# The first modulation in two column halves, and eight projection units beside the second half

## The chip, the core and the metric

The program runs on one core of a Trainium2 chip. The metric is the device time of one execution in microseconds. A core has five engines that run their own instruction queues side by side and meet at semaphores: PE (TensorE) multiplies matrices into PSUM, DVE (VectorE) and POOL (GpSimd) do elementwise work, ACT (ScalarE) does functions and copies, and SP issues the DMAs. An engine takes its instructions strictly in the order in which they are written, so an instruction that waits holds back all that stands behind it.

## What is computed

Two transformer blocks over one sequence of 256 rows and 2048 columns, all in f32. The part that matters here is the start of the first block:

```python
mod = silu(c) @ w_ada + b_ada                      # 2048 -> 6 * 2048
shift1, scale1, gate1, shift2, scale2, gate2 = split(mod, 6)
h = rms(x, norm1_w) * (1 + scale1) + shift1
proj = h @ w_in                                    # 2048 -> 4096: u, q, k, v
y_ssm = s5_mixer(u, a, dt, b, c, d, w_glu)         # a state-space layer on the first 1024 columns
y_att = dilated_attention(q, k, v)
x = x + gate1 * (concat(y_ssm, y_att) @ w_out)
# then the feed-forward network, and the second block (latent attention and a Fourier mixer)
```

## The kernel before

The kernel streams all its weights once from HBM and is written as one ordered list of instructions for each engine.

**Projection units.** A weight matrix is cut into units of 256 rows by 512 columns (512 KB). `load` (L179) brings a unit into one of eight places of the ring `raw`; ACT rounds it to fp32r into `whi` (`high`, L185), DVE subtracts to get the rest `wlo` (`low`, L191), and PE runs 12 matmuls with it (`multiply`, L198): two row groups of the weight, two halves of the sequence, three products (high by high, high by low, low by high). `whi` and `wlo` have four places each, so unit u is rounded only when unit u - 4 was multiplied. The input projection `w_in` is 64 such units: eight column chunks in the order `IN_ORDER` (L1097), each eight units long. A chunk is stored from PSUM by `in_evac` (L1100).

**First modulation.** `shift1` and `scale1` are 4096 columns of `w_ada`. SP loads them as 64 slots of 512 KB (128 rows by 1024 columns) into `start_slots`, eight places of SBUF of their own (`slots_sp`, L236). PE consumes two slots a round (`rounds_pe`, L246), 32 rounds; each round is four matmuls of 512 columns on four column groups of the array. A slot is loaded again when the round that used it is over. When all 32 rounds are done, ACT copies the sums (`set_row_act`, L275), PE turns them into columns (`set_turn_pe`, L281), and DVE adds the bias (`set_store_dve`, L295). The sums of the four pairs of columns come complete only together, with the last round.

**Turning h.** The normalized x is transposed on PE in eight steps r of two row groups (`turn_pe`, L400), DVE applies scale and shift (`turn_dve`, L412), ACT rounds to `hh` (`turn_act`, L425), and POOL subtracts to `hl` (`turn_pool`, L430). The projection starts when all eight are done (L2716).

**State-space tables.** Beside this, DVE prepares the state-space layer: parameters (L519), the table `W` (`windows_dve`, L592), which stands in `raw`, and the read tables `ct` (`reads_dve`, L607), which stand in `x` and `araw`. PE transposes `W` (`window_turn_pe`, L654) in 16 groups that ACT stores (L664), and multiplies it with `cpad` (`kt4_pe`, L669), 2 times 32 small matmuls, that ACT stores with 10 copies each (`kt4_act`, L679). SP starts the first units of `w_in` when PE has done with `W` (L2600 and L2601), since they land in the same memory.

**After the first chunks.** The first two chunks are u of the state-space layer. `u_turn_pe` (L701) transposes them, ACT and DVE copy them (`u4_act`, `u4_dve`), `ends_pe` (L731) multiplies, `ends_act` stores, and POOL runs a recurrence over the sequence (`scan`, L748), once for each half b. `y_pe` (L790) for half 0 stands behind unit 38 on PE and waits for that scan. The order of PE around the change is the body at L2702 to L2718 and `in_pe` (L1135).

## Time and profile before

| | us |
|---|---|
| median of 3 runs | 2775.4 (2774.17 to 2776.24) |
| the profiled execution | 2773.86 |
| its span | 2772.0 |
| PE busy | 2555.9 (92% of the span) |
| DVE busy | 1627.1 (59%) |
| ACT busy | 1035.2 (37%) |
| POOL busy | 204.7 (7%) |
| mean granted TensorE clock | 0.955 |

The span is the time from the first to the last instruction of the profiled execution; 1.9 us of its time lie around it. The page gives busy shares over the whole span. The change touches the first 260 us, so the stretches of that part are read apart, engine by engine in order of time. Granted clock 1.00 means 2.4 GHz and 0.50 means 1.2 GHz; a value between them is a stretch that has both.

### The profile page before, as it was taken

What the parts mean: (1) busy time and instruction counts of PE and PEld (TensorE: products, weight loads), DVE (VectorE), ACT (ScalarE), POOL (GpSimd) and SP (SyncE); (2) the same over time, 40 slices, a digit from 0 to 9 for tenths busy, and PEclk for the clock granted to TensorE, in tenths of its full rate; (3) what the DMA queues carried; (4) which work ended last, traced back from release to release, by engine and by line L of the source; (5) the groups of instructions that cost most, each with busy time, mean ns of one, the idle gap of its engine ahead of it and who ended that gap; (6) DMA issues with size and microseconds to landing.
All of it is one profiled execution on the core that took longest, in us unless ns stands there. A gap on an engine that the chain in (4) does not pass through costs nothing. (4 is left out here: it accounts for less than half of the span.)

```text
span 2772.0 us, 30616 instructions
## 1 busy us (share of the span) xinstructions
PE 2555.9 (92%) x11822; PEld 1957.1 (71%) x11822; DVE 1627.1 (59%) x1909; ACT 1035.2 (37%) x1354; POOL 204.7 (7%) x192
## 2 busy tenths in 40 slices
PE   5899887979999999999989999998949999999994
PEld 1588665547777777778768877776837777877773
DVE  8454534346777777875775674444563564744446
ACT  1343653224333333333434554443323333333331
POOL 0126800010000000000101000000020000000000
PEclk9799899989999999999999999998969999999996
DMA  9654458957999999995545643331444665745530
GB/s 392 249 152 129 131 210 321 377 206 272 339 343 342 337 343 354 357 341 180 162 152 170 203 137 99 99 122 55 158 159 143 210 225 171 270 144 153 150 118 30
DMA packets 277473, 589.24 MB, mean 213 GB/s; under 512 B 20304, under 2 KB 29264, under 8 KB 275792
## 3 DMA queue, kind: packets, MB, share of 16 engines
q1 hardware_dynamic: 277328, 587.28, 61.5%
q8 instruction: 94, 1.54, 0.2%
q14 instruction: 51, 0.42, 0.0%
HBM read 585.11 MB, written 2.10 MB: 212 GB/s over the span
## 5 line engine op out<-in xcount | busy, mean ns | idle before, releaser
L195 DVE TENSOR_TENSOR wlo<-raw,whi 128x1024 fp32r<-128x1024 f32 (+2 forms) x728 | 882.0, 1227 | 716.7 <-ACT whi L189 705.4
L189 ACT CAST whi<-raw 128x1024 fp32r<-128x1024 f32 (+2 forms) x728 | 738.0, 1024 | 978.6 <-PE psum L208 902.2
L206 PE MATMUL psum<-whi,hh 128*128 128x512 f32 (+1 forms) x2080 | 842.4, 405 | 40.1 <-DVE wlo L195 39.5
L208 PE MATMUL psum<-whi,hl 128*128 128x512 f32 (+1 forms) x2080 | 818.7, 394 | 0.0
L207 PE MATMUL psum<-wlo,hh 128*128 128x512 f32 (+1 forms) x2080 | 816.6, 393 | 0.0
L206 PEld LDWEIGHTS psum<-whi,hh 128*128 128x128 f32 x2080 | 395.6, 190 | 165.6 <-issue 76.5
L208 PEld LDWEIGHTS psum<-whi,hl 128*128 128x128 f32 x2080 | 395.0, 190 | 88.5
L207 PEld LDWEIGHTS psum<-wlo,hh 128*128 128x128 f32 x2080 | 395.8, 190 | 82.7 <-issue 2.6
L206 PE MATMUL psum<-whi,hidh 128*128 128x512 f32 x608 | 249.6, 411 | 7.7 <-DVE wlo L195 6.0
L207 PE MATMUL psum<-wlo,hidh 128*128 128x512 f32 x608 | 242.4, 399 | 0.0
L208 PE MATMUL psum<-whi,hidl 128*128 128x512 f32 x608 | 242.4, 399 | 0.0
L343 DVE SCALAR_TENSOR_TENSOR powers<-araw,cond,powers 128x512 f32<-128x512 f32 x300 | 225.2, 751 | 14.4 <-DVE powers L343 0.5
L398 POOL TENSOR_TENSOR rstd<-ms,mhalf 128x2 f32<-128x2 f32 x7 | 4.9, 699 | 2137.6 <-DVE ms L387 1843.6
L206 PEld LDWEIGHTS psum<-whi,hidh 128*128 128x128 f32 x608 | 115.5, 190 | 45.2 <-issue 16.2
L207 PEld LDWEIGHTS psum<-wlo,hidh 128*128 128x128 f32 x608 | 115.5, 190 | 29.7 <-issue 3.1
L208 PEld LDWEIGHTS psum<-whi,hidl 128*128 128x128 f32 x608 | 115.5, 190 | 28.1
L1542 DVE TENSOR_TENSOR xacc<-xacc,psum 128x1024 f32<-128x1024 f32 x68 | 82.9, 1219 | 35.8 <-PE psum L208 35.8
L266 PE MATMUL psum<-start_slots,cond_windows 128*32 128x512 f32 x256 | 49.4, 876 | 34.8 <-DMA start_slots<-in_w_ada 34.8
L408 PE MATMUL psum<-ident,xacc 128*128 128x128 f32 x128 | 29.3, 383 | 49.2 <-DVE xacc L393 29.5
L408 PEld LDWEIGHTS psum<-ident,xacc 128*128 128x128 f32 x128 | 21.0, 195 | 57.6 <-DVE xacc L393 30.0
L1635 PE MATMUL psum<-dft,ub 128*128 128x512 f32 x128 | 57.8, 594 | 2.4 <-DVE ub L1523 1.3
L428 ACT CAST hh<-h 128x512 fp32r<-128x512 f32 x32 | 19.9, 621 | 104.7 <-DVE h L421 104.7
(330 smaller groups left out, 2127.4 us busy)
## 6 DMA issues: line engine op xcount, KB each, us to landing
araw<-in_ada_w SPq DMA_DIRECT2D x128, 512.0 KB, 6.6
raw<-in_w_in_fourier SPq DMA_DIRECT2D x128, 512.0 KB, 4.3
raw<-in_w_ffn_gate SPq DMA_DIRECT2D x88, 512.0 KB, 9.6
raw<-in_w_ffn_up SPq DMA_DIRECT2D x88, 512.0 KB, 7.7
raw<-in_w_ffn_down SPq DMA_DIRECT2D x88, 512.0 KB, 10.1
raw<-in_w_in_attn SPq DMA_DIRECT2D x88, 512.0 KB, 4.1
araw<-in_w_ada SPq DMA_DIRECT2D x80, 512.0 KB, 6.4
start_slots<-in_w_ada SPq DMA_DIRECT2D x64, 512.0 KB, 7.7
```

What stands on the lines that cost most here:

```text
L189: nc.scalar.copy(whi[:, u % SPLITS, 0:kn, 0:w], raw[:, u % RING, 0:kn, 0:w]).then_inc(s_hi, 1)
L195: nc.vector.tensor_tensor(wlo[:, u % SPLITS, 0:kn, 0:w], raw[:, u % RING, 0:kn, 0:w], whi[:, u % SPLITS, 0:kn, 0:w].bitcast(F32), ALU.subt ...
L206: nc.tensor.matmul(o, ah[:, kt + k, a], h, start=(kt + k == first_kt), stop=False)
L207: nc.tensor.matmul(o, ah[:, kt + k, a], lw, start=False, stop=False)
L208: ins = nc.tensor.matmul(o, al[:, kt + k, a], h, start=False, stop=(kt + k == last_kt))
L266: ins = nc.tensor.matmul(psum[32 * g:32 * g + 32, SET_BANKS[st][0]], condz[:, vectors - 1, kt, 3 - pi:35 - pi], slot(2 * r + e)[0][:, half ...
L343: ins = nc.vector.scalar_tensor_tensor(out=dst, in0=w, scalar=s, in1=dst, op0=ALU.mult, op1=ALU.add)
L398: nc.gpsimd.tensor_tensor(rstd[:], ms[:], mhalf[:, 0:2].unsqueeze(2), ALU.pow).then_inc(s_rs, 1)
L408: ins = nc.tensor.transpose(psum[:, banks[r % 2], j * S + t * P:j * S + t * P + P], xn[:, t, kt * P:(kt + 1) * P], ident[:])
L428: nc.scalar.copy(oh[:, 2 * r:2 * r + 2], h32[:, r % 2]).then_inc(s_hh, 1)
L1542: nc.vector.tensor_tensor(o, o, psum[:, BANK[n]:BANK[n] + 2], ALU.add).then_inc(H.dv, 1)
L1635: ins = nc.tensor.matmul(psum[:, 2 + half], ub[:, t, g * S + half * P:g * S + half * P + P], dft[:, t], start=(t == 0), stop=(t == TT - 1))
```

## The change

- `PE_PAIRS` and `PE_SETS`: the 32 rounds become two sets of 16. The first set is columns 1024 to 2047 of shift and of scale, the second is columns 0 to 1023. Each set has its own row copy, turn and store (`first_columns_dve`).
- The turn of h is split: steps for row groups 8 to 15 follow the first set (`turned` swaps the halves), those for row groups 0 to 7 follow the second.
- `IN_FIRST`: of the first two chunks, the eight units on row groups 8 to 15 come first (units 0 to 7), then the eight on row groups 0 to 7 (units 8 to 15). Both chunks are open in PSUM at once.
- Homes: slots of the first modulation land in `raw`, units 0 to 7 in `araw`; `W` stands in `proj` and `bt_x` in three pieces, where its transposes also go; `cpad` stands in `proj`, and the scratch of the read tables in `ptmp`. With `W` in three pieces, each operation on it becomes three instructions.
- Order: `windows_dve` and `reads_dve` are cut into steps that stand between the units on DVE. On PE the units 0 to 7, the two `kt4_pe` and the 16 window transposes stand between the rounds 16 to 31. `in_evac` for the first two chunks waits for the tables. The u transposes move from behind units 12 and 20 to behind 16 and 22, `ends_pe` from 16 and 24 to 19 and 25.

```diff
     raw = sb(ctx, "raw", [P, RING, 2, CW])
-    a1 = ExitStack()
-    start_slots = sb(a1, "start_slots", [P, 8, 2 * CW])
-    a1.close()
     whi = sb(ctx, "whi", [P, SPLITS, 2, CW], F32R)
     wlo = sb(ctx, "wlo", [P, SPLITS, 2, CW], F32R)
...
+    def landing(u):
+
+        return araw[:, u % 4] if u < RING else raw[:, u % RING]
+
     def load(sp, u, src, w=CW, per=0, i=None):
         kn = src.shape[1]
         if i is not None or u >= RING:
             sp.wait_ge(s_lo, at(u - RING + 1, per, i))
-        sp.dma_start(raw[:, u % RING, 0:kn, 0:w], src).then_inc(s_raw[u % RING], 16)
+        elif u >= 4:
+            sp.wait_ge(s_lo, u - 3)
+        if RING <= u < 2 * RING:
+            sp.wait_ge(s_aused, 29 + (u - RING) // 2)
+        sp.dma_start(landing(u)[:, 0:kn, 0:w], src).then_inc(s_raw[u % RING], 16)
...
-    PE_PAIRS = (0, 1, 2, 3, 4, 5, 6, 7, 8, 9, 12, 13, 14, 15)
-    PE_SETS = ((0, 4, 1), (4, 2, 1), (6, 4, 1), (10, 4, 2))
-    SET_BANKS = ((6, 7), (6, 7), (6, 7), (7, 7))
+    PE_PAIRS = (1, 3, 0, 2, 4, 5, 6, 7, 8, 9, 12, 13, 14, 15)
+    PE_SETS = ((0, 2, 1), (2, 2, 1), (4, 2, 1), (6, 4, 1), (10, 4, 2))
+    SET_BANKS = ((6, 7), (6, 7), (6, 7), (6, 7), (7, 7))
...
-            t = start_slots[:, b]
+            t = raw[:, b].rearrange("p a b -> p (a b)")
...
+    def turned(k, r):
+
+        return (r + 4) % 8 if k == 0 else r
...
     btmp = pre[:, 3072:4096].rearrange("p (g c) -> p g c", g=PAIRS)
-    cpad = pre[:, 4096:6144].rearrange("p (r g c) -> p r g c", r=2, g=PAIRS)
-    ctmp = pre[:, 6144:8192].rearrange("p (g d c) -> p g d c", g=16, d=4)
-    W = rawf.rearrange("p (r g i c) -> p r g i c", r=2, g=PAIRS, i=4)
+    wtmp = pre[:, 1024:2048].rearrange("p (g c) -> p g c", g=PAIRS)
+    cpad = proj[:, :, 0:1024].rearrange("p r (g c) -> p r g c", g=PAIRS)
+    ctmp = ptmp[:].rearrange("p (g d c) -> p g d c", g=8, d=4)
+    W = (proj[:, :, 1024:3072].rearrange("p t (g r i c) -> p t g r i c", g=8, r=2, i=4),
+         proj[:, :, 3072:4096].rearrange("p t (g r i c) -> p t g r i c", g=4, r=2, i=4),
+         bt_x[:].rearrange("p (t g r) (i c) -> p t g r i c", t=1, r=2, i=4))
...
-    def windows_dve(dve, ch):
+    def windows_dve(dve, ch, i):
 
         V = nc.vector
-        br, bi = W[:, 0, :, 3], W[:, 1, :, 3]
-        for i in range(3):
-            ar, ai = (apow[:, q, :, 2 - i:3 - i].broadcast_to([P, PAIRS, 2 * GCH]) for q in range(2))
-            for q, (u, v, op) in enumerate(((br, bi, ALU.subtract), (bi, br, ALU.add))):
-                ch(V.tensor_tensor(W[:, q, :, i], ar, u, ALU.mult))
-                ch(V.tensor_tensor(btmp, ai, v, ALU.mult))
-                ch.wait()
-                ins = V.tensor_tensor(W[:, q, :, i], W[:, q, :, i], btmp, op)
+        ar, ai = (apow[:, q, :, 2 - i:3 - i].broadcast_to([P, PAIRS, 2 * GCH]) for q in range(2))
+        for q, op in enumerate((ALU.subtract, ALU.add)):
+            for n in range(3):
+                ch(V.tensor_tensor(W[n][:, :, :, q, i], of_pairs(ar, n), W[n][:, :, :, q, 3], ALU.mult))
+                ch(V.tensor_tensor(of_pairs(wtmp, n), of_pairs(ai, n), W[n][:, :, :, 1 - q, 3], ALU.mult))
+            ch.wait()
+            for n in range(3):
+                ins = V.tensor_tensor(W[n][:, :, :, q, i], W[n][:, :, :, q, i], of_pairs(wtmp, n), op)
                 ch(ins)
-                ch.wait()
-        V.tensor_copy(neg[:, 0:1], W[:, 0, 0, 0, 0:1]).then_inc(s_W, 1)
-
-    def reads_dve(dve, ch):
+            ch.wait()
+        if i == 2:
+            V.tensor_copy(neg[:, 0:1], cols[:, 0:1]).then_inc(s_W, 1)
...
     def window_turn_pe(pe, g0, g1):
-        pe.wait_ge(s_W, 1)
         for g in range(g0, g1):
-            if g >= 4:
-                pe.wait_ge(s_bt4, g - 3)
+            if g < 2:
+                pe.wait_ge(s_kt4, g + 1)
+            else:
+                pe.wait_ge(s_bt4, g - 1)
             for j in range(4):
-                ins = nc.tensor.transpose(psum[:, g % 4, j * P:(j + 1) * P], W[:, j % 2, 2 * g + j // 2]
-                                          .rearrange("p i c -> p (i c)"), ident[:])
+                ins = nc.tensor.transpose(psum[:, 4 + g % 2, j * P:(j + 1) * P], bt4(2 * g + j // 2, j % 2), ident[:])
             ins.then_inc(s_wt, 1)
...
+    IN_FIRST = ((0, 4), (1, 4), (0, 5), (1, 5), (0, 6), (1, 6), (0, 7), (1, 7),
+                (0, 0), (1, 0), (0, 1), (0, 2), (0, 3), (1, 1), (1, 2), (1, 3))
+
+    def in_unit(n):
+
+        return IN_FIRST[n] if n < 16 else (n // UPC, n % UPC)
+
     IN_ORDER = (0, 1, 2, 4, 6, 3, 5, 7)
     IN_BANK = (0, 2, 0, 2, 0, 6, 4, 6)
 
     def in_evac(act, o):
         c = IN_ORDER[o]
-        act.wait_ge(s_mm, U_IN + UPC * (o + 1))
+        act.wait_ge(s_mm, U_IN + (UPC * (o + 1) if o else 13))
+        if o < 2:
+            act.wait_ge(s_ct, 2)
+            act.wait_ge(s_ktp, 2)
         if o in (2, 4):
             act.wait_ge(s_L, o // 2)
         nc.scalar.copy(proj[:, :, c * CW:(c + 1) * CW], psum[:, IN_BANK[o]:IN_BANK[o] + 2]).then_inc(s_inev, 1)
 
     def in_load(sp, n):
-        c = IN_ORDER[n // UPC]
-        load(sp, U_IN + n, w_rows(dram["w_in"][0], 2 * (n % UPC), 2)[:, :, c * CW:(c + 1) * CW])
+        o, j = in_unit(n)
+        c = IN_ORDER[o]
+        load(sp, U_IN + n, w_rows(dram["w_in"][0], 2 * j, 2)[:, :, c * CW:(c + 1) * CW])
 
     def in_mult(pe, n):
-        o, j = n // UPC, n % UPC
-        if j == 0 and o >= 2:
+        o, j = in_unit(n)
+        if o < 2:
+            pe.wait_ge(s_hl, (j + 4) % 8 + 1)
+            multiply(pe, U_IN + n, lat(IN_BANK[o]), 2 * j, 7, first_kt=8)
+            return
...
     def in_pe(pe):
-        for n in range(43):
+        for n in range(10, 43):
             in_mult(pe, n)
             for b in range(2):
-                if n == 12 + 8 * b:
+                if n == 16 + 6 * b:
                     u_turn_pe(pe, b)
-                if n == 16 + 8 * b:
+                if n == 19 + 6 * b:
                     ends_pe(pe, b)
             if n == 38:
...
-            if n >= UPC and n % UPC == 3:
+        for n in range(12, 42):
+            if n == 15:
+                in_evac(act, 0)
+            if n >= 2 * UPC and n % UPC == 3:
                 in_evac(act, n // UPC - 1)
             for b in range(2):
-                if n == 16 + 8 * b:
+                if n == 19 + 6 * b:
                     u4_act(act, b)
-                if n == 20 + 8 * b:
+                if n == 23 + 6 * b:
                     ends_act(act, b)
             high(act, U_IN + n)
...
-                if n == 15 + 8 * b:
+                if n == 18 + 6 * b:
                     u4_dve(dve, b)
...
-        slots_sp(sp, 0, 4)
+        slots_sp(sp, 0, 2)
         sp.dma_start(x[:], dram["x"][0].rearrange("(t p) n -> p t n", p=P)).then_inc(s_x, 16)
-        sp.dma_start(pre[:, 4096:6144].rearrange("p (r n) -> p r n", r=2), dram["c_pad"].rearrange("r p n -> p r n")).then_inc(s_cpad, 16)
-        slots_sp(sp, 4, 64)
-        sp.wait_ge(s_wt, 16)
-        sp.wait_ge(s_ktp, 2)
+        slots_sp(sp, 2, 32)
+        sp.dma_start(proj[:, :, 0:1024], dram["c_pad"].rearrange("r p n -> p r n")).then_inc(s_cpad, 16)
+        in_load(sp, 0)
+        in_load(sp, 1)
+        slots_sp(sp, 32, 36)
+        in_load(sp, 2)
+        in_load(sp, 3)
+        for k in range(4, 8):
+            slots_sp(sp, 20 + 4 * k, 24 + 4 * k)
+            in_load(sp, k)
+        slots_sp(sp, 52, 64)
         in_sp(sp)
...
+        set_row_act(act, 0)
+        for r in range(4):
+            turn_act(act, 0, h32, hh, r, r + 1)
+            if r % 2:
+                high(act, U_IN + r // 2)
         act.wait_ge(s_cpad, 16)
         nc.scalar.mul(cpad[:, 1], cpad[:, 1], -1.0).then_inc(s_cneg, 1)
+        high(act, U_IN + 2)
+        high(act, U_IN + 3)
+        kt4_act(act, 0)
+        high(act, U_IN + 4)
+        high(act, U_IN + 5)
+        kt4_act(act, 1)
+        high(act, U_IN + 6)
+        high(act, U_IN + 7)
         window_turn_act(act)
-        kt4_act(act, 0)
-        kt4_act(act, 1)
-        set_row_act(act, 0)
-        act.wait_ge(s_ct, 2)
-        act.wait_ge(s_ktp, 2)
-        turn_act(act, 0, h32, hh)
+        act.wait_ge(s_hl, 4)
+        set_row_act(act, 1)
+        for r in range(4, 8):
+            turn_act(act, 0, h32, hh, r, r + 1)
+            high(act, U_IN + 4 + r)
         in_act(act)
...
-        windows_dve(dve, ch)
         norm_dve(dve, ch, 0, x, xn, True)
-        reads_dve(dve, ch)
-        set_store_dve(dve, 0)
-        dve.wait_ge(s_mcol, 1)
-        ch(nc.vector.scalar_tensor_tensor(out=mscale[:], in0=modc[:, 16:32], scalar=1.0, in1=cols[:, COLS["n1"]],
-                                          op0=ALU.add, op1=ALU.mult))
-        ch.wait()
-        turn_dve(dve, 0, h32, mscale, modc[:, 0:16])
+        windows_dve(dve, ch, 0)
+        windows_dve(dve, ch, 1)
+        first_columns_dve(dve, ch, 0)
+        for r in range(4):
+            turn_dve(dve, 0, h32, mscale, modc[:, 0:16], r, r + 1)
+            if r % 2:
+                low(dve, U_IN + r // 2)
+        windows_dve(dve, ch, 2)
+        low(dve, U_IN + 2)
+        low(dve, U_IN + 3)
+        reads_dve(dve, ch, 0, 0)
+        low(dve, U_IN + 4)
+        low(dve, U_IN + 5)
+        reads_dve(dve, ch, 0, 1)
+        low(dve, U_IN + 6)
+        low(dve, U_IN + 7)
+        first_columns_dve(dve, ch, 1)
+        for r in range(4, 8):
+            turn_dve(dve, 0, h32, mscale, modc[:, 0:16], r, r + 1)
+            low(dve, U_IN + 4 + r)
+            if r == 5:
+                reads_dve(dve, ch, 1, 0)
+        reads_dve(dve, ch, 1, 1)
         in_dve(dve, ch)
...
-        rounds_pe(pe, 0, 16)
-        for k in range(4):
-            window_turn_pe(pe, 4 * k, 4 * k + 4)
+        rounds_pe(pe, 0, 14)
+        turn_pe(pe, 0, xn, 0, 0, 2)
+        rounds_pe(pe, 14, 16)
+        set_turn_pe(pe, 0)
+        turn_pe(pe, 0, xn, 0, 2, 4)
+        for k in range(2):
             rounds_pe(pe, 16 + 2 * k, 18 + 2 * k)
+            in_mult(pe, 2 * k)
+            in_mult(pe, 2 * k + 1)
         kt4_pe(pe, 0)
-        rounds_pe(pe, 24, 27)
+        rounds_pe(pe, 20, 21)
+        in_mult(pe, 4)
         kt4_pe(pe, 1)
-        rounds_pe(pe, 27, 32)
-        set_turn_pe(pe, 0)
-        pe.wait_ge(s_kt4, 2)
-        turn_pe(pe, 0, xn, 0)
-        pe.wait_ge(s_hl, 8)
+        in_mult(pe, 5)
+        rounds_pe(pe, 21, 23)
+        in_mult(pe, 6)
+        in_mult(pe, 7)
+        for k in range(8):
+            window_turn_pe(pe, 2 * k, 2 * k + 2)
+            rounds_pe(pe, 23 + k, 24 + k)
+        rounds_pe(pe, 31, 32)
+        pe.wait_ge(s_bt4, 16)
+        turn_pe(pe, 0, xn, 0, 4, 6)
+        set_turn_pe(pe, 1)
+        turn_pe(pe, 0, xn, 0, 6, 7)
+        in_mult(pe, 8)
+        turn_pe(pe, 0, xn, 0, 7, 8)
+        in_mult(pe, 9)
```

On PE, before, from the last window transposes to the end of the rounds (L660 transposes `W`, L675 is `kt4_pe`, L266 is four matmuls a round):

```order
L660 MATMUL psum<-ident,raw 128x128 x16
L266 MATMUL psum<-start_slots,cond_windows 32x512 x8
L675 MATMUL psum<-ssm_preparation,raw 128x32 x32
L266 MATMUL psum<-start_slots,cond_windows 32x512 x12
L675 MATMUL psum<-ssm_preparation,raw 128x32 x32
L266 MATMUL psum<-start_slots,cond_windows 32x512 x20
L291 MATMUL psum<-select,h 128x4 x8
```

On PE, now, the same stretch from behind units 2 and 3 (L211 to L213 are a unit's matmuls, here units 4 to 7; L713 is `kt4_pe`, L271 the rounds, L698 the window transposes; what is left out repeats its neighbours):

```order
L713 MATMUL psum<-proj 128x32 x32
L271 MATMUL psum<-raw,cond_windows 32x512 x4
L211 MATMUL psum<-whi,hh 128x512
...
L713 MATMUL psum<-proj 128x32 x16
L713 MATMUL psum<-proj,bt_x 128x32 x16
L211 MATMUL psum<-whi,hh 128x512
...
L271 MATMUL psum<-raw,cond_windows 32x512 x8
L211 MATMUL psum<-whi,hh 128x512
...
L698 MATMUL psum<-ident,proj 128x128 x8
L271 MATMUL psum<-raw,cond_windows 32x512 x4
```

Three rounds stood between the two `kt4_pe`, and now one round and one unit do. Of the 16 rounds of the second set, nine now stand behind unit 7: eight behind two groups of window transposes each, and then the last one.

On ACT, before, from the sign change of `cpad` to the first units (L685 is `kt4_act`, L667 stores the window transposes):

```order
L2641 ACTIVATE ssm_preparation<-ssm_preparation 128x1024
L667 COPY proj<-psum 128x512 x12
L667 COPY bt_x<-psum 128x512 x4
L685 COPY kt<-psum 32x16x32 x20
L279 COPY h<-psum 128x512
L428 CAST hh<-h 128x512 x8
L189 CAST whi<-raw 128x1024 x11
```

On ACT, now (L194 is `high`, L723 `kt4_act`, L704 the window stores):

```order
L2719 ACTIVATE proj<-proj 128x1024
L194 CAST whi<-araw 128x1024 x2
L723 COPY kt<-psum 32x16x32 x10
L194 CAST whi<-araw 128x1024 x2
L723 COPY kt<-psum 32x16x32 x10
L194 CAST whi<-araw 128x1024 x2
L704 COPY proj<-psum 128x512 x12
```

The casts of units 4 and 5 stand behind the ten copies of the first `kt4`, those of units 6 and 7 behind the second ten.

On DVE, now, behind the second set of columns (L438 is a step of h, L200 `low`, L648 to L656 half a read table; before, both whole tables stood ahead of the modulation's columns):

```order
L438 TENSOR_SCALAR h<-psum,mscale,modc 128x256 x2
L200 TENSOR_TENSOR wlo<-raw,whi 128x1024
L648 TENSOR_TENSOR araw<-powers,proj 128x1024
L649 TENSOR_TENSOR pool_scan_tmp<-powers,proj 128x1024
L651 TENSOR_TENSOR araw<-araw,pool_scan_tmp 128x1024
L652 TENSOR_TENSOR araw<-powers,proj 128x1024
L654 TENSOR_TENSOR pool_scan_tmp<-powers,proj 128x1024
L656 TENSOR_TENSOR araw<-araw,pool_scan_tmp 128x1024
L438 TENSOR_SCALAR h<-psum,mscale,modc 128x256 x2
L200 TENSOR_TENSOR wlo<-raw,whi 128x1024
```

Half a read table now stands between `low` of unit 9 and the step of h that unit 11 needs, ahead of `low` of unit 10; the other half stands ahead of `low` of unit 12.

## Rows read from the trace of the kernel before

**Rows 1.** Busy time by stretch: PE, PEld, DVE, ACT, POOL; granted clock, DMA share, GB/s.

```profile
60.00:80.00 20.00, 15.50 (x129) 8.13 (x126) 19.76 (x10) 7.46 (x15) 0.00 (x0) 1.00 1.03 409
80.00:100.00 20.00, 20.00 (x122) 15.98 (x121) 9.63 (x5) 5.79 (x10) 0.00 (x0) 0.66 0.71 263
100.00:120.00 20.00, 17.11 (x95) 10.33 (x94) 2.85 (x8) 7.62 (x13) 1.97 (x2) 0.67 0.66 240
140.00:160.00 20.00, 20.00 (x89) 16.43 (x88) 9.28 (x8) 8.29 (x8) 0.00 (x0) 1.00 0.65 185
```

**Rows 2.** Timeline of PE to 115 us: start, length, instructions, idle before and releaser.

```profile
56.23 1.94 PE L266 MATMUL psum<-start_slots,cond_windows 128*32 128x512 f32 x8 [1.50 <-DMA start_slots<-in_w_ada]
...
60.48 1.93 PE L266 MATMUL psum<-start_slots,cond_windows 128*32 128x512 f32 x16
62.34 1.97 PE L660 MATMUL psum<-ident,raw 128*128 128x128 f32 x16
...
78.79 10.02 PE L675 MATMUL psum<-ssm_preparation,raw 128*128 128x32 f32 x64
88.73 5.01 PE L266 MATMUL psum<-start_slots,cond_windows 128*32 128x512 f32 x24
93.68 11.14 PE L675 MATMUL psum<-ssm_preparation,raw 128*128 128x32 f32 x64
...
111.91 1.07 PE L266 MATMUL psum<-start_slots,cond_windows 128*32 128x512 f32 x8 [0.77 <-DMA start_slots<-in_w_ada]
113.67 1.95 PE L291 MATMUL psum<-select,h 128*128 128x4 f32 x16 [0.70 <-ACT h L279]
```

**Rows 3.** Timeline of the DMA issues on SP, the last 60 slots.

```profile
5.43 102.12 SPq L244 DMA_DIRECT2D start_slots<-in_w_ada  x60
```

**Rows 4.** Timeline of DVE.

```profile
31.10 1.21 DVE L599 TENSOR_TENSOR raw<-powers,raw 128x1024 f32<-128x1024 f32 x1
...
53.09 4.84 DVE L371 BATCH_NORM_STATS2 stat<-x 128x6 f32<-128x512 f32 x8
...
62.35 2.29 DVE L616 TENSOR_TENSOR x<-powers,ssm_preparation 128x2048 f32<-128x2048 f32 x1
...
129.49 4.86 DVE L195 TENSOR_TENSOR wlo<-raw,whi 128x1024 fp32r<-128x1024 f32 x4 [1.63 <-ACT whi L189]
...
169.43 3.49 DVE L718 COPY proj<-psum 32x256 f32<-32x256 f32 x8 [4.00 <-PE psum L710]
```

**Rows 5.** Timeline of ACT.

```profile
88.84 5.90 ACT L685 COPY kt<-psum 32x512 f32<-32x512 f32 x10 [12.43 <-PE psum L675]
...
117.34 0.62 ACT L428 CAST hh<-h 128x512 fp32r<-128x512 f32 x1 [3.71 <-DVE h L421]
...
138.39 1.05 ACT L189 CAST whi<-raw 128x1024 fp32r<-128x1024 f32 x1 [1.69 <-PE psum L208]
...
154.81 1.02 ACT L1105 COPY proj<-psum 128x1024 f32<-128x1024 f32 x1 [1.64 <-PE psum L208]
...
187.52 1.93 ACT L746 COPY xacc<-psum 128x1024 f32<-128x1024 f32 x2 [7.88 <-PE psum L739]
```

**Rows 6.** Timeline of POOL: two steps of h, first and last instruction of scan 0.

```profile
121.14 2.50 POOL L433 TENSOR_TENSOR hl<-h,hh 128x512 fp32r<-128x512 f32 x2 [0.61 <-ACT hh L428]
...
189.53 0.88 POOL L767 TENSOR_TENSOR pool_scan_tmp<-powers,xacc 128x256 f32<-128x256 f32 x1 [59.67 <-ACT xacc L746]
...
253.73 1.75 POOL L786 TENSOR_TENSOR xacc<-xacc,pool_scan_tmp 128x784 f32<-128x784 f32 x1
```

**Rows 7.** Timeline of PE: unit 0, two of its matmuls, start of `y_pe` 0.

```profile
131.09 0.76 PE L206 MATMUL psum<-whi,hh 128*128 128x512 f32 x1 [5.17 <-DVE wlo L195]
...
132.50 0.63 PE L206 MATMUL psum<-whi,hh 128*128 128x512 f32 x1
132.93 0.63 PE L207 MATMUL psum<-wlo,hh 128*128 128x512 f32 x1
...
256.01 0.33 PE L799 MATMUL psum<-proj,kt 128*128 128x64 f32 x2
```

More of the change, by code:

```diff
@@ L754, in scan @@
         pool.wait_ge(s_H, 2 * b + 2)
+        pool.wait_ge(s_ct, 2)
         if b:
@@ L1123, in in_sp @@
     def in_sp(sp):
-        for n in range(8 * UPC):
+        for n in range(8, 8 * UPC):
             in_load(sp, n)
```

122 lines of the change are left out of this document (77 added, 45 removed).

## The prediction

> **What bounds the kernel now.** I read the page first: PE is busy 92% of the span, so a stretch pays only as far as it moves PE's work. Then the busy time by stretch. From 140 to 160 us PE is busy in all 20 us at granted clock 1.00 (2.4 GHz), and the DMA engines have air (share 0.65) [rows 1]. Before that three things follow each other. Until 80 us the DMA is full (share 1.00, 409 GB/s); from 80 to 120 us it is at 0.66 to 0.71 and PE is busy nearly throughout, at clock 0.66 [rows 1]. The timeline of PE says with what: the two `kt4_pe` take 10.02 and 11.14 us, and the rounds between them wait in line [rows 2]. The last round ends at 112.98 (111.91 + 1.07) [rows 2], SP having issued the last slot at 107.55 (5.43 + 102.12) [rows 3]. Third, the turn of h: from 115.6 until unit 0 starts at 131.09 PE mostly waits [rows 2, 7]. I take as the marks of the kernel before: unit 8 starts about 154.3 (the store of chunk 0, released by unit 7, starts at 154.81) [rows 5], and `y_pe` 0 starts at 256.01 [rows 7]. From there both programs have the same order, so the shift of `y_pe` 0 is the change of the time.
>
> **What the change would save.** Units 0 to 7 leave the path: 8 x 2.75 us (a unit's cast is followed by a wait of 1.69 us after 1.05 us [rows 5], and PE has no gap, so 2.75 a unit) = 22 us, and half of the turn of h. It adds to the DMA ahead of the last round 8 units of 512 KB, at 409 GB/s 1.28 us each, 10 us. That is paid if PE comes to its rounds in time. I therefore follow the three engines through the new order.
>
> **DVE up to W.** It decides when units 2 and 3 can be multiplied, since their `low` stands behind the third window step. Parameters end at 31.1 as before [rows 4]. An instruction of 1024 elements takes 1.21 us and one of 2048 takes 2.29, so the fixed part is about 0.13. The new homes add 8 instructions to the parameters and 12 to each window step: 1.0 and 1.6 us. The window steps took 22.0 us together (31.1 to 53.09), 7.3 each, now 8.9; the norm took 9.3 (53.09 to 62.35) [rows 4]. Norm done 41.4, two windows 59.2. Meanwhile round 15 is over: it was at 58.2 [rows 2], less 2.6 for `c_pad` (1 MB), which is now issued later; its row copy and turn (0.6 and 2.0 us, [rows 2]) end about 58.4. So both meet at 59, and the wait for columns is nothing. Four steps of h go at the pace of POOL, whose pair takes 2.50 us behind an idle 0.61, 3.1 us for two steps [rows 6], and two `low` (1.22 us each, [rows 4]) stand between, each behind a cast of 1.05: about 10 us, to 69. Third window step 78.0, `low` 2 done 79.2.
>
> **PE up to the last round.** From 79.2 the order on PE is serial, and each item has a row:
> units 2 and 3, 6.5 (5.5 at 2.75; at the low clock a matmul starts every 0.43 us (132.50, 132.93 [rows 7]), 5.1 a unit; PE waited just before, so I take a good third of the difference for one of them) -> 85.7;
> `kt4_pe` 0, 10.0 [rows 2] -> 95.7;
> then unit 4, whose cast stands behind the ten copies of `kt4_act` 0: 5.90 + 1.05 [rows 5] + `low` 1.22 + three handovers of 0.1 = 8.5, round 20 lying inside -> 104.2; unit 4 itself 3.9 (middle of 2.75 and 5.1) -> 108.1;
> `kt4_pe` 1, 11.1 [rows 2] -> 119.2;
> again 8.5 for `kt4_act` 1, cast and `low` of unit 6; unit 5 and rounds 21 and 22 (4.7 to 8.4 us) lie inside -> 127.7;
> units 6 and 7, 6.5 -> 134.2;
> 64 window transposes at 0.123 us (1.97 for 16 [rows 2]) 7.9, and eight rounds at 0.97 (1.93 for two) to 1.67 (5.01 for three) [rows 2], I take 1.3: 10.4 -> 152.5;
> the last round, whose slots were issued only when a place came free, 2.0 -> 154.5.
> Before it was 112.98. The slots wait all this time for PE; the DMA, which was the bound to 80 us, is idle for half of it. So the change turns a stretch in which loading hid the table work on PE into one in which table work, ACT's copies and units stand in one chain.
>
> **From the last round to unit 8.** Row copy and turn, 2.7 with handover (112.98 to 115.6 [rows 2]), columns 0.5, h 1.0, `hh` 0.62 [rows 5], cast 1.05, `low` 1.22, handovers 0.4: 7.5. Unit 8 at 162.0, 7.7 later than before.
>
> **From unit 8 to `y_pe` 0.** Both programs have units 8 to 38, two u transposes and two `ends_pe` in this stretch: 101.7 us before (154.3 to 256.0), without a wait. The new order adds:
> two single steps of transposes on PE, 1.0;
> half a read table (six instructions of 1024, 7.4) ahead of `low` 10: from unit 8's start DVE needs h 1.0, `hh` and cast and `low` 9 2.9 with handovers, table 7.4, h 1.0, `hh`, cast and `low` 10 2.9 = 15.2, while PE has units 8 and 9 and the transposes, about 7: wait 8;
> the other half ahead of `low` 12: 3.9 for `low` 11, 7.4, 1.3 = 12.6, against units 10 and 11 at 5.5 to 7.5: wait 5 to 7, I take 5;
> the u copies of DVE (3.49 [rows 4]) and a `low` now have only one unit between the transposes and the unit that needs it (4.8 - 2.75): 2.0, twice. Before there were two units, 5.5 us of cover;
> scan 0 took 66.0 us (189.53 to 255.48 [rows 6]) and ended 0.5 us before PE came to `y_pe` 0 [rows 7]: no slack. It starts 2.1 us after `ends_pe` (187.4; the store starts at 187.52 [rows 5]). PE now has three units fewer between the two: 68.5 - 8.25 + 2.0 (second u wait) = 62.3 against 68.1: wait 5.8;
> low clock after these waits, two units, half of it: 2.4.
> Together 26. Where I cost the rest at nothing (loads of units 0 to 7, `cpad` later, `high` beside), it is because these land or end before 79 us, when DVE is what is late.
>
> **Sum.** 7.7 + 25.9 = 33.5 us. The profiled execution has 2773.9 us, of which 1.9 around its span; 2773.9 + 33.5 = 2807. (The median of the runs shown is 1.5 us above that execution.)
>
> **A rule against the row.** Clock: kt4's stretch shows 0.66, although PE is busy 20.00 of 20 us, and unit 0 starts at 0.43 us a matmul after an idle stretch [rows 1, 7]. The Trainium skill, TensorE: Matmul & The Clock Gate, Part 1 (What's actually happening), says that the throttled state is the default and that activity releases it. By that rule the first unit behind every one of the six long waits would run at 1.2 GHz throughout, 2.35 us each, 14 us instead of the some 6 that stand in the sum, 2815; with the clock low all through the chain it is rival C. At unit 0 the trace agrees for the matmuls shown, and at the next units it has the pace of 2.75 again [rows 5, 7], so the sum goes by the rows.
>
> **Rivals.**
> A, faster: the loads stay the bound. PE does its table work in the gaps between slots, and the last round follows the DMA: 24 rounds were over at 78.8 before, eight more at 2.56 (two slots at 1.28) make 99.3, and the eight unit loads 109.5. Unit 8 at 117.0, 37.3 earlier; less the 25.9 behind it gives 11.4 faster, 2762. For it: PE had a gap of 1.50 us ahead of round 15 [rows 2], and a DMA share of 0.7 from 80 us on shows loading time to be had [rows 1]. Against it: the written order puts `kt4_pe` ahead of eleven rounds and behind W, which is ready at 78. It decides at the last round: break-even is 154.3 - 25.9 - 7.5 = 121, that is a chain of 42 us behind `low` 2 where I count 75.
> B, small loss: the front as I have it or 4 us shorter, and the waits behind unit 8 mostly overlapped (the table halves fall into waits for `hl`, the scan runs faster when DVE is idle): 5 + 10, 2789. For it: from 80 us on DVE was busy for only 9.63 of 20 us and then 2.85 [rows 1], so there is room beside PE's chain. Against it: the halves are placed exactly where PE needs DVE, and the scan's length is measured.
> C, larger loss, clock at 1.2 GHz through the chain: units 2 to 4, 6 and 7 at 5.1 instead of 16.9 in all +8, rounds +3, units behind the waits +6: 2824. For it: rows 1, 80 to 120.
>
> **How the numbers follow.** Forecast 0.67, A 0.11, B 0.14, C 0.08. The forecast's own range: `kt4_pe` at the high clock at best half, 5 us each, is -10; rounds at 0.97, -3; all units at 2.75, -4; extra fixed costs on DVE at nothing, -5: all together 2785, and upward rounds and units at the low clock and the second table's wait at 7: 2820. The range for 8 in 10: 2785 to 2825. Within 0.2% (5.5 us, about what can be told from no change) 0.03, a corner of A and B; faster 0.11; slower 0.86.
>
> **What would show it.** Right: the last round near 154 (over 135 in any case); PE waiting 6 to 7 us for `low` ahead of unit 4, and again ahead of unit 6 for 1 to 4; a DMA share well under 0.7 between 85 and 150; waits of 8 and 5 us ahead of units 10 and 12; 5 us ahead of `y_pe` 0, released by POOL; from there on the same distances as before. Wrong: the last round before 121, or unit 8 before 145; or equal marks at `y_pe` 0.

## The result, and the profile after

The changed kernel takes 2813.8 us (median of 4, 2812.3 to 2815.5) against 2774.8 before (median of 4, 2773.9 to 2776.2): ratio 1.014, interval 1.0123 to 1.0158. Its profiled execution has 2815.3 us and a span of 2813.5, 41.5 more than before; the forecast was 2807. One execution of the kernel with the casts ahead, below, took 11190.7 us, four times as long as any other, and is left out of its median.

| | before | after |
|---|---|---|
| span | 2772.0 | 2813.5 |
| PE busy | 2555.9 | 2567.2 |
| DVE busy | 1627.1 | 1628.8 |
| mean granted clock | 0.955 | 0.947 |
| last round ends | 112.98 | 161.27 |
| unit 8 starts | 154.62 | 168.71 |
| `y_pe` 0 starts | 256.01 | 295.64 |

PE is busy 11.3 us longer only, and the span grew by 41.5: 30.2 of the loss is idle time of PE, and the other 11.3 go with a lower mean clock and hardly with added work (11838 matmul records for 11822). 39.6 of it stand at the start of `y_pe` 0. The stretches that answer to [rows 1], same columns:

```profile
60.00:80.00 20.00, 14.25 (x67) 7.63 (x66) 16.60 (x30) 6.84 (x9) 5.03 (x4) 0.76 1.03 404
80.00:100.00 20.00, 18.49 (x94) 15.34 (x92) 6.68 (x6) 3.28 (x6) 0.00 (x0) 0.67 0.29 106
100.00:120.00 20.00, 14.93 (x73) 13.80 (x73) 9.45 (x8) 4.48 (x7) 0.00 (x0) 0.59 0.13 49
120.00:140.00 20.00, 14.32 (x54) 9.97 (x54) 2.45 (x2) 7.86 (x12) 0.00 (x0) 0.76 0.36 131
140.00:160.00 20.00, 17.76 (x132) 9.17 (x130) 0.00 (x0) 8.59 (x16) 0.00 (x0) 0.96 0.77 284
```

Read the DMA share first. To 80 us it is full in both kernels. From 80 to 140 it is 0.29, 0.13 and 0.36 now, where it was 0.71, 0.66 and 0.45 before (the first two in [rows 1], the third here; the last slot was issued at 107.55 there): the loading of the second half, which the eight units were to lie beside, all but stands still.

```profile
120.00:140.00 20.00, 13.37 (x49) 10.08 (x50) 12.00 (x17) 9.63 (x12) 8.02 (x7) 0.64 0.45 148
```

In the same stretches of the changed kernel PE is busy 18.5, 14.9 and 14.3 of 20 us, and DVE and ACT are idle for most of it: they take turns. The timeline of PE names the turns (answers to [rows 2, 7]):

```profile
78.61 0.77 PE L211 MATMUL psum<-whi,hh 128*128 128x512 f32 x1 [4.17 <-DVE wlo L200]
...
86.50 10.12 PE L713 MATMUL psum<-proj 128*128 128x32 f32 x64
...
105.07 0.76 PE L211 MATMUL psum<-whi,hh 128*128 128x512 f32 x1 [6.58 <-DVE wlo L200]
...
110.32 3.93 PE L713 MATMUL psum<-proj 128*128 128x32 f32 x32
114.09 6.82 PE L713 MATMUL psum<-proj,bt_x 128*128 128x32 f32 x32
...
129.35 0.47 PE L211 MATMUL psum<-whi,hh 128*128 128x512 f32 x1 [2.00 <-DVE wlo L200]
...
136.03 0.77 PE L211 MATMUL psum<-whi,hh 128*128 128x512 f32 x1 [3.67 <-DVE wlo L200]
...
141.28 1.20 PE L698 MATMUL psum<-ident,proj 128*128 128x128 f32 x8
...
160.20 1.07 PE L271 MATMUL psum<-raw,cond_windows 128*32 128x512 f32 x8 [1.49 <-DMA raw<-in_w_ada]
...
168.71 0.77 PE L211 MATMUL psum<-whi,hh 128*128 128x512 f32 x1 [1.99 <-DVE wlo L200]
...
184.00 0.77 PE L211 MATMUL psum<-whi,hh 128*128 128x512 f32 x1 [7.42 <-DVE wlo L200]
...
196.44 0.77 PE L211 MATMUL psum<-whi,hh 128*128 128x512 f32 x1 [4.19 <-DVE wlo L200]
...
217.63 0.50 PE L211 MATMUL psum<-whi,hh 128*128 128x512 f32 x1 [2.07 <-DVE wlo L200]
...
245.12 0.47 PE L211 MATMUL psum<-whi,hh 128*128 128x512 f32 x1 [2.66 <-DVE wlo L200]
...
295.64 0.41 PE L838 MATMUL psum<-proj,kt 128*128 128x64 f32 x2 [1.81 <-POOL xacc L825]
```

DVE is named ahead of unit 4 (6.58 us), but DVE had waited 16.91 us for ACT itself, and ACT had stood at the ten copies of `kt4`. Of ACT, then of DVE:

```profile
96.66 5.88 ACT L723 COPY kt<-psum 32x512 f32<-32x512 f32 x10 [26.50 <-PE psum L713]
102.56 1.99 ACT L194 CAST whi<-araw 128x1024 fp32r<-128x1024 f32 x2
120.94 5.88 ACT L723 COPY kt<-psum 32x512 f32<-32x512 f32 x10 [16.39 <-PE psum L713]
126.85 1.04 ACT L194 CAST whi<-araw 128x1024 fp32r<-128x1024 f32 x1
133.58 1.04 ACT L194 CAST whi<-araw 128x1024 fp32r<-128x1024 f32 x1 [5.69 <-DMA araw<-in_w_in]
```

```profile
103.69 2.36 DVE L200 TENSOR_TENSOR wlo<-araw,whi 128x1024 fp32r<-128x1024 f32 x2 [16.91 <-ACT whi L194]
```

The last cast, of unit 7, waited 5.69 us for its load. SP shows why (answers to [rows 3]):

```profile
98.55 28.81 SPq L249 DMA_DIRECT2D raw<-in_w_ada  x4
127.40 0.43 SPq L188 DMA_DIRECT2D araw<-in_w_in  x1
127.88 24.67 SPq L249 DMA_DIRECT2D raw<-in_w_ada  x12
```

The first of these rows merges slots 48 to 51. Slots 48 and 49 were issued at 98.55, when round 20 was over. Slots 50 and 51 waited until 126.56 for round 21, which stands on PE behind unit 5, and the load of unit 7 stands behind them in SP's queue. Its place in memory was free from `low` of unit 3 on, at 79.6.

### The profile page after: what moved, and what is told of

It is laid out like the page before. It is cut to its first block and busy times, and to the rows that moved or that the text cites. A ratio compares the mean times of both kernels' runs of the same rounds, so it can differ in the third digit from the quotient of the medians.

```text
span 2813.5 us, 30735 instructions
## 1 busy us (share of the span) xinstructions
PE 2567.2 (91%) x11838; PEld 1966.1 (70%) x11838; DVE 1628.8 (58%) x1969; ACT 1032.6 (37%) x1355; POOL 201.7 (7%) x192
## 5 line engine op out<-in xcount | busy, mean ns | idle before, releaser
L200 DVE TENSOR_TENSOR wlo<-raw,whi 128x1024 fp32r<-128x1024 f32 (+2 forms) x720 | 869.2, 1223 | 712.7 <-ACT whi L194 706.9
L194 ACT CAST whi<-raw 128x1024 fp32r<-128x1024 f32 (+2 forms) x720 | 727.5, 1021 | 965.1 <-PE psum L213 878.6
L211 PE MATMUL psum<-whi,hh 128*128 128x512 f32 (+1 forms) x2080 | 848.1, 408 | 71.2 <-DVE wlo L200 70.7
L213 PE MATMUL psum<-whi,hl 128*128 128x512 f32 (+1 forms) x2080 | 824.1, 396 | 0.0
L211 PEld LDWEIGHTS psum<-whi,hh 128*128 128x128 f32 x2080 | 398.9, 192 | 205.8 <-issue 106.1
L213 PEld LDWEIGHTS psum<-whi,hl 128*128 128x128 f32 x2080 | 398.2, 191 | 88.9
L211 PE MATMUL psum<-whi,hidh 128*128 128x512 f32 x608 | 250.1, 411 | 7.7 <-DVE wlo L200 6.0
L213 PE MATMUL psum<-whi,hidl 128*128 128x512 f32 x608 | 242.5, 399 | 0.0
L211 PEld LDWEIGHTS psum<-whi,hidh 128*128 128x128 f32 x608 | 115.6, 190 | 45.2 <-issue 16.2
L213 PEld LDWEIGHTS psum<-whi,hidl 128*128 128x128 f32 x608 | 115.5, 190 | 28.2
L271 PE MATMUL psum<-raw,cond_windows 128*32 128x512 f32 x256 | 44.6, 782 | 32.0 <-DMA raw<-in_w_ada 32.0
```

The lines of the kernel that those rows point to most:

```text
L194: nc.scalar.copy(whi[:, u % SPLITS, 0:kn, 0:w], landing(u)[:, 0:kn, 0:w]).then_inc(s_hi, 1)
L200: nc.vector.tensor_tensor(wlo[:, u % SPLITS, 0:kn, 0:w], landing(u)[:, 0:kn, 0:w], whi[:, u % SPLITS, 0:kn, 0:w].bitcast(F32), ALU.subtrac ...
L211: nc.tensor.matmul(o, ah[:, kt + k, a], h, start=(kt + k == first_kt), stop=False)
L213: ins = nc.tensor.matmul(o, al[:, kt + k, a], h, start=False, stop=(kt + k == last_kt))
L271: ins = nc.tensor.matmul(psum[32 * g:32 * g + 32, SET_BANKS[st][0]], condz[:, vectors - 1, kt, 3 - pi:35 - pi], slot(2 * r + e)[0][:, half ...
```

## Experiments

**One edit at a time.** Three kernels put one order of the changed kernel right; a fourth puts one thing into the kernel before. "Ratio" is always to the kernel before, with its 95% interval.

Both halves of the second read table stand behind `low` of unit 7:

```diff
         low(dve, U_IN + 7)
+        reads_dve(dve, ch, 1, 0)
+        reads_dve(dve, ch, 1, 1)
         first_columns_dve(dve, ch, 1)
...
-            if r == 5:
-                reads_dve(dve, ch, 1, 0)
-        reads_dve(dve, ch, 1, 1)
```

> The changed kernel, with both halves of the second read table moved to directly behind `low` of unit 7 on DVE. Nothing is left out. In the trace of the changed kernel DVE stands idle from 135.9 to 164.0 us there, and the two halves take 14.8 us. Theory (the halves stand in the way of `low` 10 and 12): the waits of 7.4 us ahead of unit 10 and 4.2 us ahead of unit 12 go, and with them two starts at the low clock, 2.4 us each; the pace of h and `low` on DVE (3.9 us a step against 3.3 on PE) leaves 1 to 3 us of wait. 12 to 15 us less than the changed kernel, some 2800. Rival (the turn of h behind the second set is the bound, the tables only fill it): 0 to 3 us less. Second rival (the tables delay the second set's columns): no gain or a loss.

Measured: 2795.3 us, ratio to before 1.007 (1.0055 to 1.0085), 18.5 less than the changed kernel and more than I expected. Timeline of PE:

```profile
164.83 0.76 PE L211 MATMUL psum<-whi,hh 128*128 128x512 f32 x1 [1.99 <-DVE wlo L200]
172.85 0.47 PE L211 MATMUL psum<-whi,hh 128*128 128x512 f32 x1 [0.28 <-DVE wlo L200]
176.87 0.47 PE L211 MATMUL psum<-whi,hh 128*128 128x512 f32 x1 [1.02 <-DVE wlo L200]
...
277.13 0.41 PE L838 MATMUL psum<-proj,kt 128*128 128x64 f32 x2 [0.45 <-POOL xacc L825]
```

The waits of 7.42 and 4.19 are 0.28 and 1.02, and units 10 and 12 start at 0.47 us a matmul instead of 0.77. From unit 8 to `y_pe` 0 it is 112.3 us instead of 126.9: 14.6, of which the waits are 10.3 and `y_pe`'s wait 1.4; the clock behind the waits is what is left, 2.9. The other 3.9 (unit 8 at 164.83 instead of 168.71) lie ahead of the edit, where both programs have the same order, and are not its work: in this profile the low clock lies elsewhere. Units 2 and 3 take 7.2 us (7.9 in the changed kernel), unit 4 takes 4.2 (5.25), and `kt4_pe` 1 takes 8.6 at a granted clock of 0.82 (10.6 at 0.66).

The casts of units 4 to 6 stand ahead of the copies of `kt4`:

```diff
-        kt4_act(act, 0)
         high(act, U_IN + 4)
         high(act, U_IN + 5)
-        kt4_act(act, 1)
         high(act, U_IN + 6)
+        kt4_act(act, 0)
+        kt4_act(act, 1)
         high(act, U_IN + 7)
```

> The changed kernel, with ACT's casts of units 4, 5 and 6 put ahead of the ten copies of the first `kt4_act`; the cast of unit 7 stays behind the second. Nothing is left out. Theory (PE waits for a cast that stands behind the copies): the wait of 6.6 us ahead of unit 4 goes; the one of 2.0 ahead of unit 6 goes too, but unit 7 waits for its load, which is issued when round 22 is over, so the second gain is given back in that wait: 6 to 8 us less than the changed kernel, some 2807. Rival (the low clock behind kt4_pe and DVE's read table set unit 4): under 2 us less.

Measured: 2805.5 us (median of three, 2801.8 to 2815.5), ratio 1.0102 (1.0081 to 1.0123). Timeline of PE:

```profile
124.30 0.77 PE L211 MATMUL psum<-whi,hh 128*128 128x512 f32 x1 [5.03 <-DVE wlo L200]
...
156.35 0.77 PE L211 MATMUL psum<-whi,hh 128*128 128x512 f32 x1 [1.99 <-DVE wlo L200]
...
285.95 0.41 PE L838 MATMUL psum<-proj,kt 128*128 128x64 f32 x2 [1.81 <-POOL xacc L825]
```

The wait ahead of unit 4 is gone; unit 7 now waits 5.03 us for its load, as expected. Unit 8 comes 12.4 us earlier and `y_pe` 0 9.7, and the median is 8.3 us below that of the changed kernel. The casts did hold PE up. The profiled execution is the slowest of the three, 2815.5 us. It shows nothing of the gain in its total: from `y_pe` 0 to the first product with v of the attention it takes 73.0 us, where the changed kernel has 64.6. More on that below.

The load of unit 7 stands on SP ahead of slots 48 to 51:

```diff
-        for k in range(4, 8):
+        for k in range(4, 7):
             slots_sp(sp, 20 + 4 * k, 24 + 4 * k)
             in_load(sp, k)
-        slots_sp(sp, 52, 64)
+        in_load(sp, 7)
+        slots_sp(sp, 48, 64)
```

> The changed kernel, with SP's load of unit 7 put ahead of the slots 48 to 51, on which SP waits from 79 to 127 us. Nothing is left out. Theory (the load is queued behind slots whose places come free only with round 22): the 3.7 us of idle ahead of unit 7 go and the unit starts at the high clock, 2.4 us more: 4 to 6 us less, some 2809. Rival (it only moves the wait to the last rounds, which wait for their slots anyway, 2.4 us in all in the changed kernel): under 2 us less.

Measured: 2809.5 us (2805.5 to 2818.1), ratio 1.0127 (1.0105 to 1.0149). No wait ahead of unit 7; unit 8 at 162.27, 6.4 earlier; `y_pe` 0 at 291.74, 3.9 earlier. So this load's place in the queue cost 6.4 us at unit 8. Here too the profiled execution is the slowest (2818.1), and its stretch behind `y_pe` 0 is long, 72.8 us; the median is 4.3 below the changed kernel's.

The kernel before with the new places of the u transposes and `ends_pe` alone (the diff shows PE; the copies of ACT and DVE that belong to them move as in the change):

```diff
-                if n == 12 + 8 * b:
+                if n == 16 + 6 * b:
                     u_turn_pe(pe, b)
-                if n == 16 + 8 * b:
+                if n == 19 + 6 * b:
                     ends_pe(pe, b)
```

> The kernel before, with only the places of the state-space steps taken from the change: u transposes behind units 16 and 22 instead of 12 and 20, `ends_pe` behind 19 and 25 instead of 16 and 24, and the copies of ACT and DVE with them. Theory (one unit of cover for the u copies, and scan 0 without slack): u waits of 2.1 and 2.7 us and a wait ahead of `y_pe` 0 of 2 to 6 us: 6 to 8 us more than before, some 2782. Rival (the scan speeds up beside an idle DVE and absorbs it): 2 us more. Second rival: no difference.

Measured: 2783.3 us (2780.8 to 2793.0), ratio 1.0038 (1.0024 to 1.0052). Timeline of PE:

```profile
183.32 0.54 PE L206 MATMUL psum<-whi,hh 128*128 128x512 f32 x1 [2.07 <-DVE wlo L195]
...
212.34 0.47 PE L206 MATMUL psum<-whi,hh 128*128 128x512 f32 x1 [2.62 <-DVE wlo L195]
...
262.76 0.41 PE L799 MATMUL psum<-proj,kt 128*128 128x64 f32 x2 [1.81 <-POOL xacc L786]
```

The three waits are those of the changed kernel (2.07, 2.66, 1.81). Unit 0 to `y_pe` 0 takes 133.6 us instead of 124.9: 8.7, of which 6.5 are the waits.

**The edits together.** The next kernel is the changed one with all three edits, and with the u copies of DVE one unit later:

```diff
-                if n == 18 + 6 * b:
+                if n == 19 + 6 * b:
                     u4_dve(dve, b)
```

> The changed kernel with four orders altered together: both halves of read table 2 on DVE behind low of unit 7, the casts of units 4 to 6 on ACT ahead of the copies of kt4, the load of unit 7 on SP ahead of slots 48 to 51, and the u copies of DVE one unit later. Theory (the loss is a sum of separate waits in the chain): unit 8 starts near 150 us (168.7 in the changed kernel; single edits gave -12.4 and -6.4), the waits at units 10 and 12 fall below 1.5 us, y_pe 0 starts at 261 to 263, so the whole is 2779 to 2781 when the stretch behind y_pe 0 runs at the high clock, and 8 us more, 2787 to 2789, when it runs at the low one. Rival (the waits overlap, each one removed is replaced by the next): unit 8 not before 156 and y_pe 0 not before 272, whole 2790 or more.

Measured: 2789.5 us, ratio 1.0053 (1.0041 to 1.0065). Unit 8 starts at 150.90, `y_pe` 0 at 261.94, 33.7 earlier than in the changed kernel. Up to unit 8 it gains 17.8, where the single edits of the casts and the load gave 12.4 and 6.4, together 18.8. Behind unit 8 it gains 15.9 (126.9 to 111.0), where the edit of the tables gave 14.6. They add up within 1.3 us, so these are separate waits; the rival, one wait in place of the other, is out. The fourth edit alone gains little: the two u waits (2.07 and 2.66) are gone, but `y_pe` 0 waits 5.35 for its scan instead of 1.81. The median is 24.3 us below the changed kernel's and not 33.7: in this profile `y_pe` 0 takes 20.7 us from start to end, 10.9 in the changed kernel.

Then the order on PE: rounds 20 to 31 where their slots have landed, eight of the 16 groups of window transposes behind the last round. ACT's copy of the second row of sums goes ahead of its last six stores of these groups.

```diff
-        rounds_pe(pe, 20, 21)
+        rounds_pe(pe, 20, 24)
         in_mult(pe, 4)
         kt4_pe(pe, 1)
         in_mult(pe, 5)
-        rounds_pe(pe, 21, 23)
+        rounds_pe(pe, 24, 28)
         in_mult(pe, 6)
         in_mult(pe, 7)
-        for k in range(8):
+        for k in range(4):
             window_turn_pe(pe, 2 * k, 2 * k + 2)
-            rounds_pe(pe, 23 + k, 24 + k)
-        rounds_pe(pe, 31, 32)
+            rounds_pe(pe, 28 + k, 29 + k)
+        window_turn_pe(pe, 8, 12)
+        set_turn_pe(pe, 1)
+        window_turn_pe(pe, 12, 16)
...
-        set_turn_pe(pe, 1)
```

> As the kernel with the four edits, with another order on PE: the rounds 20 to 31 stand where their slots have landed, and eight of the window transposes behind the last round, where PE would wait for the modulation's columns. Theory (the last round stands behind work that doesn't feed it): last round near 136, unit 8 near 145.5, y_pe 0 near 258, whole 2776 at the high clock behind y_pe 0, 2784 at the low one. Rival (the slots are the bound by then): the last round not before 142, PE waiting for slots, and the whole the same as with the four edits.

Measured: 2785.7 us, ratio 1.0039 (1.0026 to 1.0052). Last round 135.85, unit 8 at 148.00, `y_pe` 0 at 259.02: 2.9 earlier where I expected 4. The median is 3.8 below that of the kernel with the four edits. Slots were not the bound: PE has no wait for one behind unit 7.

And the scans one unit earlier (`u_turn_pe` at 15 + 7 * b, `ends_pe` and the copies at 18 + 7 * b, `ends_act` at 22 + 7 * b):

> As the kernel with the other order, with the u transposes, ends, their copies and so both scans one unit earlier. Theory: the scan ahead of y_pe 0 is still what is late there, so y_pe 0 comes a unit, 2.7 us, earlier: near 255, whole 2773 at the high clock behind it (equal to the kernel before). Rival: PE is late and not the scan, no difference, or 2 us worse, since the u copies come between units again.

Measured: 2782.8 us (12 runs, 2775.8 to 2786.3), ratio 1.0029 (1.002 to 1.0037). `y_pe` 0 starts at 253.70, 2.3 us earlier than in the kernel before, and still the profiled execution, 2779.0 us, is 5.2 slower, the median 9.2. What is lost in that profile lies behind that mark. Busy PE, clock, DMA share and GB/s there, in this kernel and then in the next one:

```profile
246.00:254.00 8.00, 4.93 (x24) 1.00 0.19 64
254.00:262.00 8.00, 8.00 (x44) 0.57 0.00 0
262.00:270.00 8.00, 8.00 (x40) 0.50 0.01 2
```

**The clock behind `y_pe` 0.** The granted clock falls to 0.50 (1.2 GHz) while PE is busy 8.00 of 8.00 us. At 2.4 GHz a group of `y_pe` takes 0.67 us, 16 groups 10.7; here it is 1.28 a group, 20.5 in all (timeline of PE, the kernel with the four edits):

```profile
261.94 0.66 PE L838 MATMUL psum<-proj,kt 128*128 128x64 f32 x2 [5.35 <-POOL xacc L825]
...
264.52 0.64 PE L838 MATMUL psum<-proj,kt 128*128 128x64 f32 x2
...
265.80 0.64 PE L838 MATMUL psum<-proj,kt 128*128 128x64 f32 x2
```

Next, one number changed:

```diff
-            if n == 38:
+            if n == 39:
                 y_pe(pe, 0)
```

> As the kernel with the scans one unit earlier, with y_pe 0 behind unit 39 in place of unit 38. The wait ahead of y_pe 0 goes from 3.07 us to below 0.5, and nothing else is saved, since unit 40 stands behind the same chain (y_pe 0, squares on ACT, cast, low: 7.6 us). Theory (an idle PE ahead of y_pe 0 brings it into the low clock, where it takes 20.5 us in place of 10.6): high clock, whole 2775 or less. Rival (y_pe 0 falls to the low clock by its own small matmuls, by chance, whatever stands ahead): 2780 to 2784, no difference from 2782.8.

Measured: 2773.4 us (12 runs, 2772.2 to 2778.1), ratio 0.9997 (0.9987 to 1.0007): 9.4 us less than with 38, and equal to before. Its windows, same columns:

```profile
249.00:257.00 8.00, 8.00 (x37) 1.00 0.40 122
257.00:265.00 8.00, 8.00 (x72) 1.00 0.00 0
265.00:268.00 3.00, 3.00 (x30) 1.00 0.02 5
```

So with no idle time ahead the same 48 small matmuls keep 2.4 GHz. The profiles agree with the medians: from the start of unit 38 to that of unit 40 it is 32.8 us with 38 and 23.7 with 39, 9.1 less. Over all profiles: with a wait of at most 0.45 us ahead of `y_pe` 0 it ran at 1.00 in seven of seven kernels; with 1.81 us or more it fell in six of seven (the changed kernel kept 1.00 for the first 16 us, which is all of `y_pe` 0).

One profile fixes a mark of the changed order only roughly. Four of these kernels (scans one unit earlier, and the three built on `y_pe` 0 behind unit 39) have the same order on every engine up to unit 38, and unit 38 starts at 247.72, 252.06, 254.59 and 250.35 in them. In three profiles of the old order it starts at 253.26, 253.32 and 252.84. So the 2.9 us of the other order on PE and the 2.3 us ahead of the kernel before, both read at `y_pe` 0, are within that scatter, and the medians are what they rest on.

Two more on this. `y_pe` 0 in halves with a unit between, in that kernel (there behind units 39 and 40, with the squares of ACT behind the cast of unit 40) and in the kernel before, which the diff shows:

```diff
-            if n == 38:
-                y_pe(pe, 0)
+            if n in (38, 39):
+                y_pe(pe, 0, 8 * (n - 38), 8 * (n - 38) + 8)
```

> As the one with y_pe 0 behind unit 39, but its eight groups 0 to 7 stand behind unit 39 and 8 to 15 behind unit 40, with the squares of ACT behind the cast of unit 40. At the high clock the same chain, so the same time. Theory (the small matmuls of y_pe 0 let the clock fall, a unit between gives it back): the second half runs faster than at 1.28 us a group, whole 3 to 6 us below the one with y_pe 0 behind unit 39 if that has the low clock. Rival (low clock once entered lasts through the unit too): no difference or slower by 2 to 5.

> The kernel before with y_pe 0 in two halves, behind unit 38 and behind unit 39. Before has runs from 2771 to 2782 us; if its upper ones are those with y_pe 0 at the low clock, the halves should narrow that: median 2771 to 2775, none above 2779. Rival: the spread has another cause and stays.

Measured: 2775.3 us (2769.7 to 2781.7), ratio 1.0006 (0.9997 to 1.0015), and 2776.8 (2773.1 to 2781.2), ratio 1.0012 (1.0003 to 1.0021). The first was at the high clock anyway, so it tells nothing on whether a unit gives the clock back. The second missed: its median is above the 2771 to 2775 expected, and four of its 12 runs lie above 2779. So the spread of the kernel before isn't explained by this; its cause stays open.

**A version that beats both.** Behind `y_pe` 0 PE waits 7.36 us ahead of unit 40, since ACT's squares, which wait for `y_pe` 0, stand ahead of its cast. The casts of units 40 and 41 go ahead of them, and the first transpose behind unit 41, in the last kernel at the high clock and in the kernel before:

```diff
-            if n == 40:
+            if n == 41:
                 a1_turn_pe(pe, 0)
...
             high(act, U_IN + n)
-            if n == 39:
+            if n == 41:
                 act.wait_ge(s_y, 1)
```

> As the kernel with y_pe 0 behind unit 39, with the casts of units 40 and 41 on ACT ahead of the squares that wait for y_pe 0, and the first transpose of the attention behind unit 41 in place of 40. PE waits 7.36 us ahead of unit 40 there, 3.44 ahead of that transpose and 3.76 ahead of unit 42. Theory (units 40 and 41 fill the wait for the squares, and the two casts leave that chain): the wait ahead of unit 40 goes to 0, the transpose starts 10 us behind the end of y_pe 0 in place of 15.2, all behind it 5 us earlier: 2768.5, 0.18% faster than before. Rival (unit 42 stands behind ACT's 8 exponentials anyway and they are late by other causes): within 1 us of 2773.4.

> The kernel before with the same edit of the units 40 and 41, and y_pe 0 where it was, behind unit 38. Theory: the same 4 to 5 us, 2769, so the gain has nothing to do with the changed start of the kernel, and the two versions end equal. Rival: with less idle time behind y_pe 0 the clock changes too, and the two end more than 3 us apart.

Measured: 2770.5 us, ratio 0.9983 (0.9974 to 0.9993), and 2768.4, ratio 0.9969 (0.9958 to 0.998). Timeline of PE in the first:

```profile
256.31 0.41 PE L838 MATMUL psum<-proj,kt 128*128 128x64 f32 x2 [0.30 <-POOL xacc L825]
...
270.92 0.51 PE L211 MATMUL psum<-whi,hh 128*128 128x512 f32 x1 [0.89 <-DVE wlo L200]
276.82 0.66 PE L922 MATMUL psum<-ident,xacc 128*128 128x128 f32 x4 [2.85 <-ACT xacc L910]
286.39 0.79 PE L211 MATMUL psum<-whi,hh 128*128 128x512 f32 x1 [8.91 <-DVE wlo L200]
```

Unit 42 starts 30.1 us behind the start of `y_pe` 0 (286.39 - 256.31), 35.7 without the edit. Both are faster than the kernel before, and the one without the changed start is the fastest: this gain doesn't need the change.

## Why the prediction was right

The direction and the size hold: forecast +33.5 at `y_pe` 0, measured +39.6, and 2807 against 2813.8. By its steps:

| step | predicted | measured |
|---|---|---|
| unit 2 may start | 79.2 | 78.6 |
| units 2 and 3 | 6.5 | 7.9 |
| `kt4_pe` 0 | 10.0 | 10.1 |
| to unit 4 | 8.5 | 8.45 |
| unit 4 | 3.9 | 5.25 |
| `kt4_pe` 1 | 11.1 | 10.6 |
| to unit 6 | 8.5 | 8.4 |
| units 6 and 7 | 6.5 | 11.9 |
| window transposes and rounds to the last | 20.3 | 20.0 |
| last round ends | 154.5 | 161.3 |
| last round to unit 8 | 7.5 | 7.4 |
| unit 8 to `y_pe` 0, beyond before | 25.9 | 25.5 |

- **One chain in place of an overlap**: right in each long term. The waits for ACT's ten copies are 8.45 and 8.4 us; moving the casts shows that they caused them.
- **Units 6 and 7** are the term that failed: 5.4 too small. I cost "the rest at nothing (loads of units 0 to 7 ...)" because they would land before 79 us. The load of unit 7 was issued at 127.40. I had followed the order on PE, ACT and DVE and not on SP, where it stands behind two slots (50 and 51) that need round 21, which stands behind unit 5. The wait was 3.67; the rest is the low clock.
- **The clock** was mis-sized, some 6 us in the sum. At 2.75 us a unit at 2.4 GHz, units 2 and 3 hold 2.4 of it, unit 4 2.5, units 6 and 7 2.7 (11.9 - 5.5 - 3.7), and behind unit 8 it is 6.4 (25.5 less the waits of 7.42, 4.19, 2.07, 2.66 and 1.81 and 1.0 for the transposes): 14.0. The Trainium skill, TensorE: Matmul & The Clock Gate, Part 1 (What's actually happening), has the low clock as what an idle PE falls back to; worked out by it I had 14 us and 2815. The trace agrees: units 4, 7, 8, 10 and 12, all behind long waits or nearly idle stretches, start at 0.76 or 0.77 us. I should have taken the rule. It doesn't say everything: `y_pe` 0 ran at 0.50 with PE busy in 8.00 of 8.00 us.
- **Window transposes and rounds** came out at 20.0 for 20.3 by luck: the nine rounds took 1.07 us each and not 1.3 and 2.0 for the last, 2.8 less, and PE waited 2.4 us for slots.
- **Behind unit 8** the sum came out, 25.5 for 25.9, and that too is luck: a wait 4.0 too long stands against a clock term 4.0 too small. The terms as written add up to 26.2, and unit 8 of the kernel before starts at 154.62 and not at the 154.3 that I took from the store. The table waits were 7.42 and 4.19 for 8 and 5, the u waits 2.07 and 2.66 for 2.0 each, but `y_pe`'s wait was 1.81 for 5.8. I took the scan at its old length, 66.0 us. It took 62.95 (232.55 to 295.50). Three units fewer lie beside it, and each `low` beside it is slower than the 1.22 us alone. By line on DVE, for the time of the scan, in the kernel before and after:

```profile
L195 DVE TENSOR_TENSOR wlo<-raw,whi 128x1024 fp32r<-128x1024 f32 x20 | 36.3, 1856 | 27.7 <-ACT whi L189 27.7
```

```profile
L200 DVE TENSOR_TENSOR wlo<-raw,whi 128x1024 fp32r<-128x1024 f32 x17 | 27.6, 1646 | 30.0 <-ACT whi L194 29.9
```

  3 `low` fewer, 3.0 us of scan less, about 1 us each. The other kernels bear it out: scan 0 takes 62.8 to 63.7 us with 17 `low` beside it, 63.9 to 64.1 with 18, 64.7 to 64.8 with 19, 66.0 with 20 and 66.8 with 21. The Trainium skill, GPSIMD Engine Reference, Specifications, says that POOL's way into SBUF is shared with DVE, and that instructions of DVE with two inputs from SBUF contend for it. `low` is one, and the trace agrees, on DVE's side in `low`'s mean.
- **Rivals.** A needed a last round before 121; it came at 161, and even in the best order not before 132.83. B needed overlapping waits behind unit 8; they added up. It was right that the scan gets shorter, by 3.0 us. C had the clock low through the chain: it was 0.59 to 0.76 from 80 to 140, but 0.96 for the transposes and rounds behind, and the time stayed 10 below its 2824.
- **The last step**, that from `y_pe` 0 on the distances are as before, held to 1.9 us, and this was luck. The wait of 1.81 us ahead of `y_pe` 0 is also in three other kernels, the two with the casts and the load moved and the kernel before with the new places, and in their profiles the clock fell in `y_pe` 0 and some 7 us were lost. The sum had no term for that.

Not explained: these 1.9 us of the span, which lie behind `y_pe` 0. Matched instruction by instruction, the shift is 38.2 us at 391 us of the kernel before, 40.8 at 649 and 41.5 at the end.

## What to carry to other kernels

Work placed "beside" a load hides nothing if the load's next slot waits for the same engine: follow the free place of memory as well as the bytes, on the loading queue too, and look at the DMA share. When copies of one job and casts of another share an in-order engine, the casts that the bottleneck waits for go first. A short wait ahead of many small matmuls can cost more than its length through the clock (here 9.4 us for one of 3.07); move them to where their operands are ready. And when a single edit moves marks by a few us, compare several executions: the profiled one may be the slowest.

## What the runs showed of the hardware

- A wait of 1.81 to 5.35 us ahead of `y_pe` 0 (matmuls of 63 and 64 columns) was followed by 1.2 GHz in six of seven profiles, although PE was then busy throughout, 20.5 us for 10.7. Removing the wait took 9.4 us off. The wait itself was 3.07 us in the kernel from which it was removed.
- A DVE subtraction of 1024 elements takes 1.22 us alone and 1.86 on average while POOL runs its scan, and the scan is 3.0 us shorter with three of them fewer; from 17 to 21 of them it goes from 62.8 to 66.8 us.
- The 24 instructions that the split homes add to two window steps on DVE cost less than I took: these steps take 16.2 us (40.42 to 56.65), not 17.8.
